# Cross attention on one core: the turned tile taken back at the start of each step

## The reference, cut to what matters

```python
def memory_cross_attention(h, m, w_cq, w_ckv, w_co):
    q = (h @ w_cq).reshape(b, s, X_HEADS, X_DH)
    k, v = jnp.split(m @ w_ckv, 2, axis=-1)
    sc = jnp.einsum('bshd,bmhd->bhsm', q, k).astype(jnp.float32) * (X_DH ** -0.5)
    p = jax.nn.softmax(sc, axis=-1)
    o = jnp.einsum('bhsm,bmhd->bshd', p.astype(v.dtype), v).reshape(b, s, D_MODEL)
    return o @ w_co
```

## Time and profile before

| | before |
|---|---|
| median of 3 runs | 1571.56 us |
| profiled execution | 1573.0 us |
| its span (first to last instruction) | 1571.0 us |
| TensorE busy | 98% of the span |
| VectorE, ScalarE, GpSimd busy | 57%, 39%, 43% |
| granted TensorE clock, mean | 0.995 |
| edited loop, first scores to last weighting | 451.3 to 516.8 us |

### The profile page before, as it was taken

How to read it: one execution, slowest core, us unless ns; L and a number is a source line. 1 busy time by engine, 2 the same in 40 slices (tenths; PEclk the granted TensorE clock), 3 DMA queues, 4 the chain that set the end, 5 groups by cost and what they waited for, 6 DMA issues and landing times.

```text
span 1571.0 us, 19620 instructions
## 1 busy us (share of the span) xinstructions
PE 1547.2 (98%) x7696; PEld 1249.9 (80%) x7696; DVE 887.7 (57%) x1351; ACT 614.2 (39%) x991; POOL 677.5 (43%) x316
## 2 busy tenths in 40 slices
PE   8999999999999999999999999999989999999998
PEld 6877767788988788888877788887878888888887
DVE  3437685675225568775345735477687772534425
ACT  5624443573444532222322444643524322222223
POOL 3543223354842445555543443244534544444441
PEclk9999999999999999999999999999999999999999
DMA  5532221243541458773333234221233333333331
GB/s 169 175 94 59 62 68 51 80 126 94 175 134 54 135 190 263 252 254 99 97 101 108 83 92 149 68 70 49 71 121 108 94 94 96 104 96 94 95 100 60
DMA packets 264719, 176.17 MB, mean 112 GB/s; under 512 B 8177, under 2 KB 242291, under 8 KB 264372
## 3 DMA queue, kind: packets, MB, share of 16 engines
q1 hardware_dynamic: 251212, 146.15, 31.4%
q10 hardware_dynamic: 12856, 26.66, 4.9%
q0 software_dynamic: 560, 2.12, 0.4%
HBM read 170.65 MB, written 4.25 MB: 111 GB/s over the span
## 4 chain that ended last, share of the span: by engine, by line
PE 94%; DVE 3%; ACT 2%; issue 1%; DMA 0%; SPq 0%; ACTq 0%; DVEq 0%
PE ps L1319 52%; PE ps L1331 12%; PE ps L1345 6%; PE ps L1774 5%; PE ps L1480 3%; PE ps L1494 2%; PE ps L1485 2%; PE ps L1550 1%; PE ps L1414 1%; PE ps L1536 1%; PE ps L2006 1%; PE ps L1661 1%; PE ps L1641 1%; PE ps L1573 1%; PE ps L1522 1%
## 5 line engine op out<-in xcount | busy, mean ns | idle before, releaser
L693 POOL TENSOR_TENSOR WL<-raw,WH 128x1024 fp32r<-128x1024 f32 (+2 forms) x268 | 624.4, 2332 | 866.2 <-ACT WH L740 866.0
L740 ACT ACTIVATE WH<-raw 128x1024 fp32r<-128x1024 f32 (+2 forms) x268 | 273.4, 1020 | 697.5 <-PE ps L1319 477.2
L1319 PE MATMUL ps<-hH,WH 128*128 128x512 f32 x704 | 175.2, 391 | 0.0
L1319 PE MATMUL ps<-hL,WH 128*128 128x512 f32 x704 | 173.9, 389 | 0.0
L1319 PE MATMUL ps<-hH,WL 128*128 128x512 f32 x704 | 173.9, 389 | 0.0
L1319 PEld LDWEIGHTS ps<-hH,WH 128*128 128x128 f32 x704 | 131.4, 188 | 30.9 <-issue 3.9
L1319 PEld LDWEIGHTS ps<-hL,WH 128*128 128x128 f32 x704 | 132.1, 188 | 27.5
L1319 PEld LDWEIGHTS ps<-hH,WL 128*128 128x128 f32 x704 | 132.1, 188 | 27.4
L1331 PE MATMUL ps<-hH,WH 128*128 128x512 f32 x272 | 112.7, 414 | 0.1
L1331 PE MATMUL ps<-hH,WL 128*128 128x512 f32 x272 | 106.8, 393 | 0.0
L1331 PE MATMUL ps<-hL,WH 128*128 128x512 f32 x272 | 106.3, 391 | 0.0
(11 more groups left out here) (608 smaller groups left out, 2787.2 us busy)
## 6 DMA issues: line engine op xcount, KB each, us to landing
raw<-in_w_in_dram SPq DMA_DIRECT2D x64, 512.0 KB, 3.7
raw<-in_w_mlp_dram SPq DMA_DIRECT2D x64, 512.0 KB, 3.9
raw<-in_w_gate_up_dram SPq DMA_DIRECT2D x44, 512.0 KB, 3.8
ada_w<-in_w_ada_dram ACTq DMA_DIRECT2D x40, 512.0 KB, 4.7
raw<-in_w_out_dram SPq DMA_DIRECT2D x16, 512.0 KB, 3.9
raw<-in_w_ckv_dram SPq DMA_DIRECT2D x16, 512.0 KB, 3.8
raw<-in_w_down_dram SPq DMA_DIRECT2D x16, 448.0 KB, 3.6
raw<-in_w_cq_dram SPq DMA_DIRECT2D x8, 512.0 KB, 4.2
```

What stands on the lines that cost most here:

```text
L693: pool.tensor_tensor(WL[un.slot][:, 0:s_.kt, 0:n], raw[un.slot][:, 0:s_.kt, 0:n], WH[un.slot][:, 0:s_.kt, 0:n].bitcast(F32), ALU.subtract) ...
L740: act.activation(WH[un.slot][:, 0:s_.kt, 0:n], raw[un.slot][:, 0:s_.kt, 0:n], ACT.Copy).then_inc(high_done, 1)
L1319: ins = pe.matmul(dst, w[un.slot][:, q, 0:m], a[:, q, :], start=(k == 0), stop=(k == 3 * kt - 1))
```

## The change

On ScalarE and VectorE the turned tile of item s-2 comes first in step s, ahead of Exp or maximum of the new item, for all s. At step 16 the third output's copies and remainders come ahead of turned tile 14. TensorE, GpSimd and the DMA queues have the same instructions in the same order.

```diff
--- before.py
+++ after.py
@@ -506,6 +506,7 @@
             return vec[:, c + i:c + i + 1]
 
         A_ITEMS, B_ITEMS, C_ITEMS = A_HEADS * ST, B_HEADS * ST, X_HEADS * ST
+        TURN_FIRST = 2
         AB = A_ITEMS + B_ITEMS
         HEAD_STEPS = (22, 26, 30, 34)
         STEPS = AB + 4
@@ -991,14 +992,18 @@
                 high(at["cq", i].u + SLOTS)
             act.wait_ge(stat_r, stat_no["cross"] + 1)
             for s_ in range(C_ITEMS + 2):
+                if s_ == C_ITEMS:
+                    high_c(s_ // 4 - 2)
+                if s_ >= TURN_FIRST:
+                    keep_c(s_ - 2)
                 if s_ < C_ITEMS:
                     exp_c(s_)
-                if s_ >= 2:
+                if 2 <= s_ < TURN_FIRST:
                     keep_c(s_ - 2)
                 for un in cross_ended(s_):
                     query_high(un)
                     high(un.u + SLOTS)
-                if s_ >= 8 and s_ % 4 == 0:
+                if s_ in (8, 12):
                     high_c(s_ // 4 - 2)
             high_c(X_HEADS - 1)
 
@@ -2480,15 +2485,19 @@
 
             each("cq", query_tile, 0, 3)
             for s_ in range(C_ITEMS + 2):
+                if s_ == C_ITEMS:
+                    out_c(s_ // 4 - 2)
+                if s_ >= TURN_FIRST:
+                    turn_low(s_ - 2)
                 if s_ < C_ITEMS:
                     max_c(s_)
                 if 1 <= s_ <= C_ITEMS:
                     norm_c(s_ - 1)
                 for un in cross_ended(s_ - 1):
                     query_tile(un)
-                if s_ >= 2:
+                if 2 <= s_ < TURN_FIRST:
                     turn_low(s_ - 2)
-                if s_ >= 8 and s_ % 4 == 0:
+                if s_ in (8, 12):
                     out_c(s_ // 4 - 2)
             out_c(X_HEADS - 1)
```

## The result

| | before | after |
|---|---|---|
| median | 1572.34 us (4 runs, 1571.56 to 1573.19) | 1590.67 us (4 runs, 1587.72 to 1592.05) |
| ratio | | 1.0114, 95% interval 1.0102 to 1.0126 |
| profiled execution, span | 1573.0, 1571.0 us | 1592.05, 1590.1 us |
| edited loop, first scores to last weighting products | 451.3 to 515.9: 64.6 us | 450.8 to 535.2: 84.4 us |

The loop is measured here to the start of its last `pcH` by `vcH` product (515.93 before), 0.8 us ahead of the end of its last product, 516.8, in the table of the kernel before.

A forecast was written before the change was run, and what follows sets the result against it. The prediction took TensorE, 94% of the chain of waits, as the bound. Delays 3.3 + 2.8 + 2.8 + 0.6 + 1.1 + 1.3 = 11.9 us plus 1.7 us of clock, 13.6 us, gave 1585.2 us, range 1581.0 to 1589.0.

The forecast's parts named there:

- three waits: Scores of items 4, 8 and 12 wait for query remainders: prices 3.3, 2.8, 2.8 us; idle 3.1, 2.6, 2.6.
- The three small terms: Item 8's transposes 0.6 us later, item 12's transposes 1.1 us, and the loop's end 1.3 us.
- The sum of 11.9 us: Edited loop: six delays, three at head starts and three small ones, add 11.9 us before any clock loss.
- its variant of 11.0 us: Same sum if weight loads are already in place, saving 0.15 us at each of six restarts; not adopted.
- 491.68, 503.56 and 513.34: Forecast times in us of item 8's transposes, item 12's transposes and the end of item 15's normalising.
- the lower bound of 9.4: Least total delay of the loop: restarts off by 0.15 or 0.06 us, small terms at half; 9.4 us.
- one loss in three stops: TensorE's clock drops to half for 3.4 us after one of three head-start stops: 1.7 us; chance 0.37.
- The rival with two or three losses: Clock lost after two or three head-start stops, or once for 6.8 us: 1586.9 to 1588.6 us; chance 0.20.
- The run of 2.47 us: At head starts, from ScalarE's turned-tile copy to the end of VectorE's query remainder: 2.47 us.
- Given back: TensorE's wait for VectorE at 1148 absorbs up to 4.9 us of the delay: 1580.3 us; chance 0.09.
- faster: Head starts have no stops, and waits of 0.55 and 1.23 us vanish: 1569.8 us; chance 0.04.
- nothing: The order does nothing, since copies wait for the same transposes anyway: 1571.6 us; chance 0.03.

The follow-up runs named there:

- the step-12 kernel: Changed kernel with its tile-first threshold at step 12 in place of 2; median +1.2 us to before, ratio 1.0008, loop 67.1 us.
- the kernel with extra matmuls and the later subtraction: Changed kernel with extra matmuls in the three head-start waits and GpSimd's slab subtractions held until that step's normalising; median +10.3 us to before, loop 76.7 us.
- the kernel with extra matmuls: Changed kernel with 28, 20 and 24 extra TensorE matmuls ahead of the scores of items 4, 8 and 12; median +13.9 us to before, loop 78.6 us.
- the subtraction later: Changed kernel with GpSimd's five slab subtractions held back until that step's item is normalised; median +16.0 us to before, loop 81.0 us.
- the one-step kernel: Kernel before, tile first only in step 13, third output ahead of tile 14 but behind item 15's normalising; median 1569.39 us, ratio 0.9982, loop 63.2 us.
- the kernel with the query remainder first: Changed kernel with VectorE's query remainder put back ahead of the same step's turned tile; median +5.6 us to before, ratio 1.0036, loop 70.3 us.

## Why the prediction was right and where it was wrong

**The waits: right.** The placement of the query remainder behind the turned tile costs three waits, where the prediction put them and, without the collisions, at its sizes (3.09, 2.66, 2.66 us). The three small terms (1.1 and 1.3 checked together, as 2.5 us, by the step-12 kernel; 0.6 by its row of 0.35 us plus a restart) held too. The 1.1 was worked out at item 12's transposes and stood elsewhere: there is no wait there, and 1.45 us ahead of the output pieces of item 14, as the prediction's list of signs had it. The sum of 11.9 us measured 12.1 in the kernel with extra matmuls and the later subtraction, so its variant of 11.0 us, with weights in place at each restart, did not come out. Slips in its additions are small: 491.68, 503.56 and 513.34 come out 0.02 lower from their own terms, and the lower bound of 9.4, whose working isn't given, at about 9.5.

**The step that failed: the clock.** The prediction took "one loss in three stops", 1.7 us. There were three losses, one of them twice as long, 5.8 us by the loop of the kernel with extra matmuls. With the 1.9 us of the next paragraph this closes the sum: 12.1 + 5.8 + 1.9 = 19.8. The rival with two or three losses was the right one, with its 0.20; its upper price, 5.1 us, was short because it took either three short losses or one long one, not both. The rows had shown that a wait of 1.23 us keeps the clock and one of 4.9 us doesn't; the prediction weighed stops of 2.6 and 3.1 us as if they lay nearer to the first, and no row spoke for that. The small-matmul stretch at 1205, which lost the clock with TensorE 100% busy, showed that the clock can fall without a long wait, and should have weighed more.

**The term left out: GpSimd.** The run of 2.47 us came from a stretch where GpSimd was idle. In its timeline of before it starts 0.02 us after the normalising of the earlier trace rows has ended (462.99 + 0.35 = 463.34):

```profile
463.36 2.39 POOL L693 TENSOR_TENSOR WL<-raw,WH 128x1024 fp32r<-128x1024 f32 x1 [7.80 <-ACT WH L740]
```

The prediction named the slab copies of ScalarE as moved by 1.7 us and as hidden, and did not ask what GpSimd, which starts on each, would then run beside. That was 1.9 us (78.6 against 76.7). The Trainium skill has the rule, "SBUF — State Buffer", section "SBUF: two separate sides": VectorE and GpSimd share a pair of ports under an exclusive lock, and where the VectorE instruction runs in a two-port mode or has two SBUF inputs, whichever of the two engines starts first keeps the other out until its instruction ends. The trace agrees as far as it goes: each long normalising, from SBUF to SBUF, ends 0.14 to 0.16 us after the subtraction it overlaps. In which mode the normalising ran no run here shows.

**Given back, faster, nothing:** all three fell. The wait at 1148 is 4.9 us as before, since VectorE's run there moves with TensorE.

## What to carry to other kernels

When an instruction moves behind one that waits for the bound engine's latest work, look at everything queued behind it for something that same engine needs next; here the place of one 0.68 us remainder made 14 of the loop's 20 us, the clock's part with it. Price each new stop of TensorE with its clock as well, and try the dependent instruction in front first. A move that delays a copy also delays the engine that starts on it, so check what that one will then run beside. And an order that pays in one step of a loop need not pay in the next: the same edit in step 13 alone removed a wait.

## What was not expected of the hardware

- Waits of 2.66 us sufficed for TensorE's clock to fall to 1.2 GHz for 3.4 us (at 490 in the changed kernel, at 489 with the subtraction later), and once, at the same 2.66 us, it did not fall. In the waits of 3.09 and 3.88 us it fell while TensorE still waited, at about 465.4 and 466.5 us, some 2 and 2.6 us after its last product.
- The same unedited code lost the clock in some profiles and not in others: the wait of 4.9 us near 1150 cost 6.8 us of half clock before and 3.4 us in the step-12 kernel, and the small matmuls at 1205 lost it before and not in the one-step kernel.
- A normalising from SBUF to SBUF on VectorE (128x256, 0.35 us) took up to 1.21 us beside GpSimd's 2.4 us subtraction, and is shown as busy all that time. The subtraction kept its 2.34 to 2.40 us. Maximum (0.41 us, from PSUM) and its scaling (0.21 us, one column) were not lengthened beside it.
- Restarts cost beyond the idle shown, an estimate: 14.3 us of idle less the 1.8 of before are 12.5, and 19.8 - 12.5 - 5.8 of clock leaves 1.5 us over six additional waits, some 0.25 us each. In the kernel with the query remainder first, at full clock, the waits grew by 4.3 us and the loop by 5.7, so 1.4 us over five additional waits.
